# mLSTM scan of a hybrid decoder layer: the state unpadded, the query product per head in alternating halves of TensorE's array, key sums for two heads and score row sums for a row tile in one matmul each

## The chip, the cores and the metric

One core of a Trainium2 chip runs one launch of one layer of a hybrid decoder: TensorE for the matmuls, VectorE, ScalarE and GpSimd beside it, DMA queues for the weights. The metric is the device time of a launch in microseconds (us), the median of some runs; lower is better.

## The reference, cut to what matters

The sequence is 256 tokens, the model width 2048. Behind an RMSNorm and one wide projection stand three token mixers (forgetting attention, gated DeltaNet, mLSTM), whose outputs are gated, summed and projected; a gated MLP with a short convolution and a final RMSNorm follow. The change is in the mLSTM, a scan over 4 chunks of 64 tokens, for 8 heads with keys and queries of 64 and values of 128 numbers. In shortened form:

```
def step(carry, xs):                 # per chunk of L = 64 tokens
    C, n, m = carry                  # C (h, 64, 128), n (h, 64)
    ...
    Sm = Wd * qk_i                   # masked, weighted scores, 64 x 64 per head
    num = w_inter[..., None] * einsum('bhld,bhde->bhle', q_i, C) + einsum('bhls,bhse->bhle', Sm, v_i)
    den = w_inter * einsum('bhld,bhd->bhl', q_i, n) + sum(Sm, axis=-1)
    h = num / maximum(abs(den), exp(-m_r))[..., None]
    C = w_inter[..., -1, None, None] * C + einsum('bhl,bhld,bhle->bhde', wL, k_i, v_i)
    n = w_inter[..., -1, None] * n + einsum('bhl,bhld->bhd', wL, k_i)
```

## The kernel before

The weights stream through a ring of four slots in chunks of 128 x 1024 numbers. ScalarE rounds each to a high part `w_hi`, VectorE or GpSimd takes the low part `w_lo`, and TensorE multiplies both with the activations `xnT`, in groups of 128 x 512 outputs. These are the groups `ps<-w_hi,xnT` and `ps<-w_lo,xnT` in the rows. They make up most of the program.

The token mixers are cut into small *items*, which `plan_items()` places behind numbered weight chunks, so that TensorE does a projection, then an item, then a projection. The order of all items is fixed when the program is built. Items take turns in two pairs of PSUM banks, banks 4 and 5 and banks 6 and 7; `item_done` and `item_free` hand them over between TensorE and the engine that reads the result. `item(k)` is a function of each engine's program and issues what that engine does for item k.

Items of the mLSTM scan, per chunk c (rows `r` = partitions 0 to 63 for an even chunk and 64 to 127 for an odd one; `tt` = c // 2 is the row tile of 128 tokens):

- `qc` (from chunk 1 on): query times state. The queries `mq` hold a pair of heads on the partitions (even head on 0 to 63, odd head on 64 to 127). The state `c_st` is padded: for each pair of heads a block of 2 x 128 columns, in which the columns of the even head are zero on the odd head's partitions and the other way round. So one matmul with 128 rows and 256 columns gives both heads of a pair, 4 of them per chunk.
- `dc`: what the chunk adds to the state and to the norm. First, from chunk 1 on, 4 matmuls of queries with the key-sum state `n_st` (2 columns). Then for each of the 8 heads: the row sums of the scores `smt` (a matmul with a column of ones, 1 column), the sum of the weighted keys `mkt` (1 column), and keys times values `mkt`, `mv` (128 columns). All three have 64 rows and 64 output partitions: `smt` writes the partitions `r`, the other two write those of the head's half. VectorE then forms `den`, scales the state by `w_last` into `c_n` (two operations, one per half of the partitions) and adds the new part into `c_st` (two more), and raises `mstate_ready`, for which the next `qc` waits.
- `sv` (after an odd chunk, two weight chunks later): scores times values for the whole row tile.

The next `qc` follows four weight chunks behind a `dc`. The names in a row such as `ps<-c_st,mq` are written tile <- moving operand, stationary operand. A shape as `128*64` is rows x columns of the array that a matmul takes up. Each fp32 matmul of the program stands as two records in the trace, each with a weight load of its own, so "x8" in a row is 4 matmuls of the code.

```
                elif name == "qc":
...
                    for j in range(H // 2):
                        last = mm(oh[r, 2 * j:2 * j + 2, :], mq[:, j, c * L:c * L + L], c_st[:, j, :, :])
```

Of the kernel before, what the change touches and what calls it, by code (L numbers as in the profile page):

```python
# [14 lines left out]
ALU = mybir.AluOpType  # L15
# [5 lines left out]
P = 128  # L21
# [3 lines left out]
NT = SEQ // P  # L25
# [143 lines left out]
def hybrid_layer_kernel(nc, x, norm_mix_g, w_in, fox_f_bias, gdn_conv_w, gdn_a_log, gdn_dt_bias, gdn_norm_g,  # L169
# [3 lines left out]
    with ctx:  # L173
        cursor = [nc.sbuf_base + (-nc.sbuf_base) % 2048]

        def small(name, shape, dt=F32):
            n = 4
            for s in shape[1:]:
                n *= s
            at = cursor[0]  # L180
            cursor[0] += n + (-n) % 64
            return nc.alloc_sbuf_tensor_at(name, shape, dt, offset=at)
# [48 lines left out]
        c_kw = small("c_kw", [P, NT, H])  # L231
        w_last = small("w_last", [P, NT, 2, H])
        n_st = small("n_st", [P, H // 2, 2])
# [65 lines left out]

        c_st = part("c_st", 0, [P, H // 2, 2, HD])  # L300
        c_n = part("c_n", 2, [P, H // 2, HD])
        mt1 = part("mt1", 1, [P, H, HD])
# [135 lines left out]

        BLOCKS = (slice(0, L), slice(L, P))

        def within(ap, b):
# [134 lines left out]
        def _(pe):  # L576
# [86 lines left out]
            def item(k):  # L663
# [152 lines left out]
                elif name == "qc":  # L816
                    c, = args
                    r, tt = chunk_rows(c)
                    pe.wait_ge(S["mstate_ready"], c)
                    for j in range(H // 2):  # L820
                        last = mm(oh[r, 2 * j:2 * j + 2, :], mq[:, j, c * L:c * L + L], c_st[:, j, :, :])
                elif name == "dc":
# [6 lines left out]
                    if c:  # L829
                        for j in range(H // 2):  # L830
                            mm(o[r, 1, 2 * j:2 * j + 2], mq[:, j, c * L:c * L + L], n_st[:, j, :])
                    for h in range(H):
                        g = slice(L * (h % 2), L * (h % 2) + L)
                        j = h // 2
                        mm(o[r, 1, 8 + h:9 + h], smt[r, tt, h, r], ones[r, 0:1])
                        mm(o[g, 1, 16 + j:17 + j], mkt[r, tt, h, :], ones[r, 0:1])
                        last = mm(o[g, 0, j * P:j * P + P], mkt[r, tt, h, :], mv[r, tt, h, :])
                elif name == "sv":
# [454 lines left out]
        def _(dve):  # L1293
# [50 lines left out]
            def item(k):  # L1344
# [137 lines left out]
                elif name == "mtail":  # L1482
                    item_written(dve, k)
                    dve.tensor_copy(w_last[:, :, :, :].rearrange("p t b h -> p b t h"),
                                    o[:, 0, 16:48].rearrange("p (b t h) -> p b t h", b=2, t=2))
                    tt_(c_kw[:, :, :], vs[:, :, :], o[:, 0, 0:16].rearrange("p (t h) -> p t h", t=2),
# [21 lines left out]
                elif name == "qc":  # L1508
# [3 lines left out]
                    if c == 2:  # L1512
                        item_read(dve, "sv", 0)
                    tt_(mt1[r, :, :], oh[r], over_free(w_int8[r, tt, :], HD), ALU.mult).then_inc(free, 1)
                elif name == "dc":
# [4 lines left out]
                    if c == 0:  # L1520
                        chain(dve.tensor_copy(den[r, tt, :], o[r, 1, 8:16]))
                        dve.wait_ge(S["ml_zero"], 3)
                        for b in range(2):
                            g = slice(L * b, L * b + L)
                            dve.tensor_copy(n_st[g, :, b], o[g, 1, 16:20])
                            ins = dve.tensor_copy(c_st[g, :, b, :], dcs[g])
                        chain(ins)
                    else:
                        item_read(dve, "qc", c)
                        chain(tt_(den[r, tt, :], o[r, 1, 0:8], w_int8[r, tt, :], ALU.mult))  # L1530
                        chain(tt_(den[r, tt, :], den[r, tt, :], o[r, 1, 8:16], ALU.add))
                        for b in range(2):
                            g = slice(L * b, L * b + L)
                            wl = w_last[g, tt, c % 2, :].rearrange("p (j b) -> p j b", b=2)[:, :, b]
                            tt_(c_n[g, :, :], c_st[g, :, b, :], over_free(wl, HD), ALU.mult)
                            chain(tt_(n_st[g, :, b], n_st[g, :, b], wl, ALU.mult))
                        for b in range(2):
                            g = slice(L * b, L * b + L)
                            tt_(n_st[g, :, b], n_st[g, :, b], o[g, 1, 16:20], ALU.add)
                            ins = tt_(c_st[g, :, b, :], c_n[g, :, :], dcs[g], ALU.add)  # L1540
                        chain(ins)
                    dve.sem_inc(S["mstate_ready"], 1)
# [334 lines left out]
        def _(pool):  # L1877
# [54 lines left out]
            def item(k):  # L1932
# [31 lines left out]
                elif name == "vbc":  # L1964
                    tt, = args
                    if tt == 0:
                        item_written(pool, k)
                        for t in (n_st[:, :, :], c_st[:, :, :, :], mt1[:, :, :]):
                            pool.memset(t, 0.0).then_inc(S["ml_zero"], 1)
# [78 lines left out]
```

## Time and profile before

| What | us |
|---|---|
| Median of 3 runs | 1839.68 |
| Lowest and highest of them | 1837.96, 1841.13 |
| Span of the profiled execution (first to last instruction) | 1838.6 |
| TensorE busy in it, matmuls | 1817.3 (99%) |
| TensorE weight loads, beside the matmuls | 1567.1 (85%) |
| VectorE, ScalarE, GpSimd busy | 1065.3, 826.7, 434.0 |

The profile is of one execution; its page gives a span and no separate time, and the span lies 1.1 us under the median of the runs. A timeline row gives the start from the beginning of the span, the length of the group, the engine, the line, the operation with its tiles, the array shape, the shape of the output and the number of records.

### The profile page before, as it was taken

To read this page: it belongs to the slowest core of one execution; us is meant where nothing else is said; L and a number is where in the kernel's file an instruction comes from. 1 tells how busy PE (TensorE), PEld (TensorE's weight loads), DVE (VectorE), ACT (ScalarE), POOL (GpSimd) and SP (SyncE) were. 2 spreads that over 40 slices of the span, in tenths; PEclk is the share of its full clock that TensorE was granted. 3 is DMA by queue.
4 is the path that set the end of the run, shared out by engine and by line. 5 is a ranking of instruction groups with operands and counts; after the bars stand their busy time and mean duration, and the time that the engine had idled before them with its cause. 6 is when DMAs were issued, how large, how long until landed. Compare 5 with 4: busy or idle time off the path is not lost.

```text
span 1838.6 us, 28288 instructions
## 1 busy us (share of the span) xinstructions
PE 1817.3 (99%) x10949; PEld 1567.1 (85%) x10949; DVE 1065.3 (58%) x1279; ACT 826.7 (45%) x910; POOL 434.0 (24%) x242
## 2 busy tenths in 40 slices
PE   8999999999999999999999999999999999999997
PEld 6888898888888888888888878888888888888886
DVE  5678736366555755555556366666666666633334
ACT  5555333436433544444444354444444444444444
POOL 5222431121221222222222232222222222222223
PEclk9999999999999999999999999999999999999999
DMA  6666544444554566666667646666666666665663
GB/s 199 178 180 180 148 116 135 130 138 139 165 154 121 155 207 182 197 192 184 188 188 244 202 148 185 183 190 190 189 184 190 188 191 184 213 195 186 196 194 134
DMA packets 263436, 324.58 MB, mean 177 GB/s; under 512 B 16779, under 2 KB 230213, under 8 KB 262725
## 3 DMA queue, kind: packets, MB, share of 16 engines
q1 hardware_dynamic: 263366, 323.58, 58.2%
q8 instruction: 51, 0.84, 0.2%
q14 instruction: 19, 0.16, 0.0%
HBM read 321.45 MB, written 2.10 MB: 176 GB/s over the span
## 4 chain that ended last, share of the span: by engine, by line
PE 97%; DVE 1%; ACT 1%; DMA 0%; issue 0%; DVEq 0%; SPq 0%; ACTq 0%
PE ps L578 96%; PE ps L659 0%; DVE xs L1808 0%; DMA x_in<-in_x_dram 0%; PE ps L690 0%; PE ps L872 0%; PE ps L849 0%; ACT w_hi L376 0%; ACT p L994 0%; DVE x L1791 0%; ACT junk L994 0%; ACT x_sq L994 0%; PE ps L955 0%; DVE fmax L1448 0%; DVE p L1443 0%
## 5 line engine op out<-in xcount | busy, mean ns | idle before, releaser
L376 ACT ACTIVATE w_hi<-raw 128x1024 fp32r<-128x1024 f32 x601 | 635.1, 1059 | 877.5 <-PE ps L578 866.4
L381 DVE TENSOR_TENSOR w_lo<-raw,w_hi 128x1024 fp32r<-128x1024 f32 x450 | 561.5, 1254 | 490.7 <-ACT w_hi L376 489.8
L578 PE MATMUL ps<-xnT,w_hi 128*128 128x512 f32 (+1 forms) x2960 | 748.7, 394 | 0.7 <-issue 0.7
L381 POOL TENSOR_TENSOR w_lo<-raw,w_hi 128x1024 fp32r<-128x1024 f32 x151 | 366.7, 2428 | 1305.6 <-ACT w_hi L376 1305.6
L578 PEld LDWEIGHTS ps<-xnT,w_hi 128*128 128x128 f32 (+1 forms) x2960 | 532.4, 189 | 99.4 <-issue 1.5
L578 PEld LDWEIGHTS ps<-xnT,w_lo 128*128 128x128 f32 (+1 forms) x2960 | 403.9, 190 | 29.0
L578 PE MATMUL ps<-xnT,w_lo 128*128 128x256 f32 (+1 forms) x2960 | 415.2, 282 | 0.0
L578 PE MATMUL ps<-w_hi,xnT 128*128 128x512 f32 x1408 | 356.4, 392 | 0.0
L578 PEld LDWEIGHTS ps<-w_hi,xnT 128*128 128x128 f32 x1408 | 261.8, 188 | 54.7 <-issue 0.7
L578 PE MATMUL ps<-w_lo,xnT 128*128 128x512 f32 x704 | 192.2, 389 | 0.0
L578 PEld LDWEIGHTS ps<-w_lo,xnT 128*128 128x128 f32 x704 | 132.1, 188 | 27.8 <-DVE w_lo L381 0.2
L1342 DVE TENSOR_REDUCE upre<-ps 128x512 f32<-128x1024 f32 x44 | 53.9, 1224 | 136.9 <-PE ps L578 136.9
L1848 DVE SCALAR_TENSOR_TENSOR uacc<-upre,fconv_c,uacc 128x256 f32<-128x256 f32 x176 | 77.5, 481 | 11.8 <-DVE uacc L1846 0.2
L1342 DVE TENSOR_REDUCE g_sum<-ps 128x512 f32<-128x1024 f32 x24 | 29.3, 1221 | 28.9 <-PE ps L578 28.9
L1342 DVE TENSOR_REDUCE g_pr<-ps 128x512 f32<-128x1024 f32 x24 | 29.3, 1221 | 28.2 <-PE ps L578 28.2
L994 ACT ACT_TABLE_LOAD x30 | 38.5, 1283 | 1.3 <-PEq L2036 0.8
L994 ACT ACTIVATE g_sig<-g_sum,cols 128x256 f32<-128x256 f32 x48 | 21.9, 503 | 26.9 <-DVEq L1624 21.8
L1606 DVE SCALAR_TENSOR_TENSOR acc<-pre,conv_c,acc 128x256 f32<-128x256 f32 x72 | 32.5, 492 | 1.3
L578 PE MATMUL ps<-y_gdn,w_hi 128*128 128x512 f32 x128 | 32.1, 392 | 0.0
L578 PE MATMUL ps<-y_ml,w_hi 128*128 128x512 f32 x128 | 32.1, 392 | 0.0
L578 PE MATMUL ps<-y_fox,w_hi 128*128 128x512 f32 x128 | 32.0, 392 | 0.0
L1929 POOL TENSOR_TENSOR nlv<-nt,level 128x512 f32<-128x512 f32 x12 | 18.9, 1586 | 39.7 <-PE ps L578 33.5
(325 smaller groups left out, 1031.0 us busy)
## 6 DMA issues: line engine op xcount, KB each, us to landing
raw<-in_w_in_dram SPq DMA_DIRECT2D x256, 512.0 KB, 3.8
raw<-in_w_up_dram SPq DMA_DIRECT2D x176, 512.0 KB, 3.9
raw<-in_w_down_dram SPq DMA_DIRECT2D x88, 512.0 KB, 4.4
raw<-in_w_out_dram SPq DMA_DIRECT2D x32, 512.0 KB, 4.5
raw<-in_w_fox_proj_dram SPq DMA_DIRECT2D x16, 512.0 KB, 4.2
raw<-in_w_gdn_proj_dram SPq DMA_DIRECT2D x16, 512.0 KB, 4.3
raw<-in_w_ml_proj_dram SPq DMA_DIRECT2D x16, 512.0 KB, 4.0
x_in<-in_x_dram SPq DMA_DIRECT2D x4, 512.0 KB, 6.0
```

The costliest lines, as they stand in the source:

```text
L376: act.activation(w_hi[:, s, 0:n], raw[:, s, 0:n], ACT.Copy).then_inc(hi_ready[s], 1)
L381: eng.tensor_tensor(w_lo[:, s, 0:n], raw[:, s, 0:n], w_hi[:, s, 0:n], ALU.subtract).then_inc(lo_ready[s], 1)
L578: return pe.matmul(o, l, r, start=start, stop=stop)
L994: return act.activation(o, i, fn, **kw)
L1342: return dve.tensor_reduce(dst, ps[:, b0:b0 + 2, :].rearrange("p b (s t) -> p b t s", s=2), AX.X, ALU.add)
L1606: ins = dve.scalar_tensor_tensor(acc[:, b, :], pre[:, b, j:j + SEQ], conv_c[:, j, n:n + 1], acc[:, b, :], ALU.mult, ALU.add)
L1848: ins = dve.scalar_tensor_tensor(uacc[:, w, b, :], src, cw, uacc[:, w, b, :], ALU.mult, ALU.add)
L1929: pool.tensor_tensor(nlv[:, tt, :, :], nt_[:, tt, :, :], over_heads(level[:, lv, 0:L], H), ALU.mult).then_inc(S["level_ready"], 1)
```

## The change

Five things, all in the mLSTM scan:

1. `c_st` loses its padding (128 x 4 x 128 in place of 128 x 4 x 2 x 128), and `c_n` goes. GpSimd no longer clears `c_st`.
2. `qc` is 8 matmuls, one per head, of 64 rows, 64 output partitions and 128 columns, with even heads on array rows 0 to 63 and odd heads on 64 to 127 in turn. Even heads write one PSUM bank and odd heads the other (`by_half`).
3. The score row sums are taken once for a row tile, in its even chunk, with 128 rows and 128 output partitions: 8 matmuls in chunks 0 and 2, none in 1 and 3.
4. The key sums are taken for a pair of heads at a time: 4 matmuls per chunk with 64 rows and 128 output partitions, in place of 8 with 64.
5. VectorE scales and adds the state over all 128 partitions at once and in place: 2 operations of 128 x 512 in place of 4 of 64 x 512. `w_last` holds only the heads of a partition's half.

The numbers of keys-times-values matmuls and of queries-times-`n_st` matmuls stay as they were, and so does the order of items and weight chunks.

```diff
-        c_st = part("c_st", 0, [P, H // 2, 2, HD])
-        c_n = part("c_n", 2, [P, H // 2, HD])
+        c_st = part("c_st", 0, [P, H // 2, HD])
...
+        def by_half(oh):
+
+            return oh.rearrange("p (b j) d -> p j b d", b=2)
...
                     pe.wait_ge(S["mstate_ready"], c)
-                    for j in range(H // 2):
-                        last = mm(oh[r, 2 * j:2 * j + 2, :], mq[:, j, c * L:c * L + L], c_st[:, j, :, :])
+                    for h in range(H):
+                        g = BLOCKS[h % 2]
+                        last = mm(by_half(oh)[r, h // 2, h % 2, :], mq[g, h // 2, c * L:c * L + L], c_st[g, h // 2, :])
...
                     if c:
                         for j in range(H // 2):
                             mm(o[r, 1, 2 * j:2 * j + 2], mq[:, j, c * L:c * L + L], n_st[:, j, :])
+                    if c % 2 == 0:
+                        for h in range(H):
+                            mm(o[:, 1, 8 + h:9 + h], smt[:, tt, h, :], ones[:, 0:1])
+                    for j in range(H // 2):
+                        mm(o[:, 1, 16 + j:17 + j], mkt[r, tt, 2 * j:2 * j + 2, :].rearrange("p b l -> p (b l)"), ones[r, 0:1])
                     for h in range(H):
-                        g = slice(L * (h % 2), L * (h % 2) + L)
                         j = h // 2
-                        mm(o[r, 1, 8 + h:9 + h], smt[r, tt, h, r], ones[r, 0:1])
-                        mm(o[g, 1, 16 + j:17 + j], mkt[r, tt, h, :], ones[r, 0:1])
-                        last = mm(o[g, 0, j * P:j * P + P], mkt[r, tt, h, :], mv[r, tt, h, :])
+                        last = mm(o[BLOCKS[h % 2], 0, j * P:j * P + P], mkt[r, tt, h, :], mv[r, tt, h, :])
...
                         item_read(dve, "qc", c)
-                        chain(tt_(den[r, tt, :], o[r, 1, 0:8], w_int8[r, tt, :], ALU.mult))
-                        chain(tt_(den[r, tt, :], den[r, tt, :], o[r, 1, 8:16], ALU.add))
-                        for b in range(2):
-                            g = slice(L * b, L * b + L)
-                            wl = w_last[g, tt, c % 2, :].rearrange("p (j b) -> p j b", b=2)[:, :, b]
-                            tt_(c_n[g, :, :], c_st[g, :, b, :], over_free(wl, HD), ALU.mult)
...
+                        dve.tensor_tensor(den2[r, tt, :], o[r, 1, 0:8], w_int8[r, tt, :], ALU.mult)
+                        if c % 2 == 0:
+                            dve.tensor_copy(den[:, tt, :], o[:, 1, 8:16])
+                        wl = w_last[:, tt, c % 2, :]
+                        tt_(c_st[:, :, :], c_st[:, :, :], over_free(wl, HD), ALU.mult)
...
+                        chain(tt_(c_st[:, :, :], c_st[:, :, :], dcs, ALU.add))
                     dve.sem_inc(S["mstate_ready"], 1)
```

On TensorE, the items `qc` and `dc` of chunk 1 stood as follows before, counted in matmuls of the code, between two projections (the numbers behind the names are the program's buffer numbers):

```order
L578 MATMUL ps<-w_lo_51,xnT_52 128x512 x4
L578 MATMUL ps<-c_st_147,mq_141 64x256 x4
L578 MATMUL ps<-n_st_94,mq_141 64x2 x4
L578 MATMUL ps<-ones_54,smt_146 64x1
L578 MATMUL ps<-ones_54,mkt_143 64x1
L578 MATMUL ps<-mv_144,mkt_143 64x128
```

The last three rows repeat for each of the 8 heads, and a projection follows. In the changed kernel the same place reads:

```order
L581 MATMUL ps<-w_lo_51,xnT_52 128x512 x4
L581 MATMUL ps<-c_st_147,mq_141 64x128 x8
L581 MATMUL ps<-n_st_94,mq_141 64x2 x4
L581 MATMUL ps<-ones_54,mkt_143 128x1 x4
L581 MATMUL ps<-mv_144,mkt_143 64x128 x8
L581 MATMUL ps<-w_hi_50,xnT_52 128x512 x8
```

The interleaved one-column matmuls have become runs of one kind, and the score sums have left this odd chunk. Chunk 2, an even one, holds them for its row tile, on TensorE of the changed kernel:

```order
L581 MATMUL ps<-c_st_147,mq_141 64x128 x8
L581 MATMUL ps<-n_st_94,mq_141 64x2 x4
L581 MATMUL ps<-ones_54,smt_146 128x1 x8
L581 MATMUL ps<-ones_54,mkt_143 128x1 x4
L581 MATMUL ps<-mv_144,mkt_143 64x128 x8
```

Before, chunk 2 was the same as chunk 1. Now it has 8 score sums with 128 output partitions between the `n_st` matmuls and the key sums.

## Rows read from the trace of the kernel before

**Rows 1.** the page: span, busy time of each engine, chain by engine
```profile
span 1838.6 us, 28288 instructions
...
PE 1817.3 (99%) x10949; PEld 1567.1 (85%) x10949; DVE 1065.3 (58%) x1279; ACT 826.7 (45%) x910; POOL 434.0 (24%) x242
...
PE 97%; DVE 1%; ACT 1%; DMA 0%; issue 0%; DVEq 0%; SPq 0%; ACTq 0%
...
```

**Rows 2.** windows: length; busy (x) PE, PEld, DVE, ACT, POOL; granted clock; DMA share; GB/s
```profile
...
1087.40:1090.80 3.40, 1.09 (x8) 0.86 (x8) 3.27 (x3) 2.20 (x5) 3.40 (x3) 1.00 0.21 56
1090.80:1097.70 6.90, 5.36 (x19) 4.00 (x20) 6.90 (x8) 5.01 (x8) 3.05 (x3) 0.51 0.15 51
...
545.00:595.00 50.00, 50.00 (x365) 41.27 (x364) 28.25 (x54) 15.93 (x15) 7.17 (x3) 1.00 0.45 129
...
```

**Rows 3.** timeline of TensorE, chunk 0: start, length, group xrecords
```profile
...
533.81 1.07 PE L578 MATMUL ps<-w_lo,xnT 128*128 128x512 f32 x4
534.81 0.27 PE L578 MATMUL ps<-ones,smt 64*64 64x1 f32 x2
...
537.25 2.14 PE L578 MATMUL ps<-w_hi,xnT 128*128 128x512 f32 x8
...
```

**Rows 4.** timeline of TensorE, chunk 1
```profile
...
548.40 1.94 PE L578 MATMUL ps<-c_st,mq 128*64 128x256 f32 x8
550.18 0.58 PE L578 MATMUL ps<-n_st,mq 128*64 128x2 f32 x8
550.68 0.21 PE L578 MATMUL ps<-ones,smt 64*64 64x1 f32 x1
550.69 0.21 PE L578 MATMUL ps<-ones,mkt 64*64 64x1 f32 x1
...
553.10 2.11 PE L578 MATMUL ps<-w_hi,xnT 128*128 128x512 f32 x8
...
```

**Rows 5.** timeline of TensorE, chunk 2
```profile
...
566.00 1.94 PE L578 MATMUL ps<-c_st,mq 128*64 128x256 f32 x8
...
570.72 2.11 PE L578 MATMUL ps<-w_hi,xnT 128*128 128x512 f32 x8
...
```

**Rows 6.** timeline of TensorE, chunk 3
```profile
...
581.83 1.94 PE L578 MATMUL ps<-c_st,mq 128*64 128x256 f32 x8
...
586.52 2.11 PE L578 MATMUL ps<-w_hi,xnT 128*128 128x512 f32 x8
...
```

**Rows 7.** timeline of TensorE, short matmuls on the whole array
```profile
...
493.41 1.07 PE L578 MATMUL ps<-w_lo,xnT 128*128 128x512 f32 x4
494.32 0.28 PE L578 MATMUL ps<-m_t,sel 128*128 128x8 f32 x2
494.45 2.08 PE L578 MATMUL ps<-w_hi,xnT 128*128 128x512 f32 x8
...
507.19 0.60 PE L578 MATMUL ps<-w_int,sel 128*128 128x16 f32 x4
507.63 1.07 PE L849 MATMUL ps<-ident,gvt 128*128 128x128 f32 x8
...
```

**Rows 8.** timeline of TensorE, item u (64x64 tiles) and item wt
```profile
...
324.32 2.00 PE L578 MATMUL ps<-xmt,kbg 64*128 64x64 f32 x32
326.25 2.11 PE L578 MATMUL ps<-w_hi,xnT 128*128 128x512 f32 x8
...
334.08 1.96 PE L578 MATMUL ps<-gvt,xmt 64*64 64x128 f32 x32
335.97 2.14 PE L578 MATMUL ps<-w_hi,xnT 128*128 128x512 f32 x8
...
```

**Rows 9.** timeline of TensorE, item mqk (row halves)
```profile
...
517.74 1.16 PE L578 MATMUL ps<-mq,mk 64*128 64x128 f32 x16
518.83 1.09 PE L659 MATMUL ps<-ident,bm 128*128 128x128 f32 x8
...
```

**Rows 10.** timeline of VectorE, end of chunk 1's state update
```profile
...
557.27 0.20 DVE L1546 RECIPROCAL rd<-den 64x8 f32<-64x8 f32 x1
...
```

More of the change, by code:

```diff
@@ L231, in hybrid_layer_kernel @@
         c_kw = small("c_kw", [P, NT, H])
-        w_last = small("w_last", [P, NT, 2, H])
+        w_last = small("w_last", [P, NT, 2, H // 2])
         n_st = small("n_st", [P, H // 2, 2])
@@ L1483, in item @@
                     item_written(dve, k)
-                    dve.tensor_copy(w_last[:, :, :, :].rearrange("p t b h -> p b t h"),
-                                    o[:, 0, 16:48].rearrange("p (b t h) -> p b t h", b=2, t=2))
+                    for b, g in enumerate(BLOCKS):
+                        dve.tensor_copy(w_last[g, :, :, :].rearrange("p t c j -> p c t j"),
+                                        o[g, 0, 16:48].rearrange("p (c t j b) -> p c t j b", c=2, t=2, b=2)[:, :, :, :, b])
                     tt_(c_kw[:, :, :], vs[:, :, :], o[:, 0, 0:16].rearrange("p (t h) -> p t h", t=2),
@@ L1513, in item @@
                         item_read(dve, "sv", 0)
-                    tt_(mt1[r, :, :], oh[r], over_free(w_int8[r, tt, :], HD), ALU.mult).then_inc(free, 1)
+                    w8 = w_int8[r, tt, :].rearrange("p (j b) -> p j b", b=2)
+                    tt_(mt1[r, :, :].rearrange("p (j b) d -> p j b d", b=2), by_half(oh)[r],
+                        w8.unsqueeze(3).to_broadcast([L, H // 2, 2, HD]), ALU.mult).then_inc(free, 1)
                 elif name == "dc":
@@ L1520, in item @@
                     if c == 0:
-                        chain(dve.tensor_copy(den[r, tt, :], o[r, 1, 8:16]))
-                        dve.wait_ge(S["ml_zero"], 3)
-                        for b in range(2):
-                            g = slice(L * b, L * b + L)
+                        dve.tensor_copy(den[:, tt, :], o[:, 1, 8:16])
+                        dve.wait_ge(S["ml_zero"], 2)
+                        for b, g in enumerate(BLOCKS):
                             dve.tensor_copy(n_st[g, :, b], o[g, 1, 16:20])
-                            ins = dve.tensor_copy(c_st[g, :, b, :], dcs[g])
@@ L1527, in item @@
-                        chain(ins)
+                        chain(dve.tensor_copy(c_st[:, :, :], dcs))
                     else:
                         item_read(dve, "qc", c)
-                        chain(tt_(den[r, tt, :], o[r, 1, 0:8], w_int8[r, tt, :], ALU.mult))
-                        chain(tt_(den[r, tt, :], den[r, tt, :], o[r, 1, 8:16], ALU.add))
-                        for b in range(2):
-                            g = slice(L * b, L * b + L)
-                            wl = w_last[g, tt, c % 2, :].rearrange("p (j b) -> p j b", b=2)[:, :, b]
-                            tt_(c_n[g, :, :], c_st[g, :, b, :], over_free(wl, HD), ALU.mult)
-                            chain(tt_(n_st[g, :, b], n_st[g, :, b], wl, ALU.mult))
@@ L1537, in item @@
-                        for b in range(2):
-                            g = slice(L * b, L * b + L)
+                        dve.tensor_tensor(den2[r, tt, :], o[r, 1, 0:8], w_int8[r, tt, :], ALU.mult)
+                        if c % 2 == 0:
+                            dve.tensor_copy(den[:, tt, :], o[:, 1, 8:16])
+                        wl = w_last[:, tt, c % 2, :]
+                        tt_(c_st[:, :, :], c_st[:, :, :], over_free(wl, HD), ALU.mult)
+                        for b, g in enumerate(BLOCKS):
+                            ins = tt_(n_st[g, :, b], n_st[g, :, b], wl[g], ALU.mult)
@@ L1539, in item @@
+                        chain(ins)
+                        tt_(den[r, tt, :], den[r, tt, :], den2[r, tt, :], ALU.add)
+                        for b, g in enumerate(BLOCKS):
                             tt_(n_st[g, :, b], n_st[g, :, b], o[g, 1, 16:20], ALU.add)
-                            ins = tt_(c_st[g, :, b, :], c_n[g, :, :], dcs[g], ALU.add)
-                        chain(ins)
+                        chain(tt_(c_st[:, :, :], c_st[:, :, :], dcs, ALU.add))
                     dve.sem_inc(S["mstate_ready"], 1)
@@ L1967, in item @@
                         item_written(pool, k)
-                        for t in (n_st[:, :, :], c_st[:, :, :, :], mt1[:, :, :]):
+                        for t in (n_st[:, :, :], mt1[:, :, :]):
                             pool.memset(t, 0.0).then_inc(S["ml_zero"], 1)
```

## The prediction

> **What bounds the kernel now.** I read the page first: TensorE is busy for 1817.3 of 1838.6 us and makes up 97% of the chain that ended last [rows 1]. Then the windows: from 545 to 595 us, where the scan lies, TensorE is busy for all 50.00 us, VectorE for 28.25, at full granted clock [rows 2]. So within the scan nothing but TensorE's own time counts: a microsecond less in an item starts the next projection a microsecond sooner, and what VectorE saves counts for nothing. Last I read TensorE's timeline chunk by chunk, from the item's first record to the first record of the next projection: chunk 0 takes 537.25 - 534.81 = 2.44 us [rows 3], chunk 1 553.10 - 548.40 = 4.70 [rows 4], chunk 2 570.72 - 566.00 = 4.72 [rows 5], chunk 3 586.52 - 581.83 = 4.69 [rows 6]. Together 16.55 us, 0.9% of the span: the change can touch no more than that. Within chunk 1, `qc` takes 550.18 - 548.40 = 1.78 us for 8 records, the `n_st` products 0.50 for 8, and the rest 553.10 - 550.68 = 2.42 us for 48 records (16 each of score sums, key sums and keys times values) [rows 4].
>
> **Prices from the rows.** Durations in the rows overlap, so a price is the distance between starts.
> (a) A record of few columns on 64 array columns: 0.50 / 8 = 0.06 us [rows 4].
> (b) A record of few columns on 128 array columns: the four `w_int` records go from 507.19 to 507.63, 0.11 us each, at 16 columns [rows 7]. That the columns of the weights set it and not the rows is seen in item wt: 32 records of 64 rows on 128 array columns, in alternating row halves, take 326.25 - 324.32 = 1.93 us, 0.12 per pair, though they stream 64 columns only [rows 8].
> (c) Pairs of 64x64 tiles side by side at 128 columns: item u has 32 records in 335.97 - 334.08 = 1.89 us [rows 8]. Half is 0.95; the ends don't halve, so I take 1.0 for 16 records. Item mqk says the same for row halves that write the same PSUM partitions in two banks, as the new `qc` does, but on 128 array columns: 16 records in 518.83 - 517.74 = 1.09 us [rows 9].
> (d) Changing the array's shape: four `w_lo` records are followed after 534.81 - 533.81 = 1.00 us by a 64x64 record [rows 3] and after 494.32 - 493.41 = 0.91 by one on the whole array [rows 7]. So 0.09 us per change of shape.
>
> **The Trainium skill on this.** The rows (b) and (a) stand at 0.11 and 0.06 us for a record of few columns, so a merged sum on 128 array columns costs what two on 64 cost [rows 4, 7]. The Trainium skill ("TensorE: Matmul & The Clock Gate", section "LDWEIGHTS (loading the stationary operand)") states that a weight load lasts as long as its columns at 1.2 GHz, whatever the rows: 107 ns for 128. The trace agrees, with 112 ns; it speaks against merging sums. By its figure the 64 new sum records would be 64 x 0.005 = 0.3 us cheaper than by the rows, an estimate of -0.9 us in all in place of the -0.6 below.
>
> **The change, part by part.**
> *`qc`* (chunks 1 to 3): 8 records of 256 columns become 16 of 128 columns in two row halves. By (c) 1.0 us in place of 1.78, so -0.78 a chunk. The next group, the `n_st` products, now follows a change of shape at its head, which I put at 0.05 more in it: 0.55. This is the estimate nearest to (d); the end of `qc` is in the 1.0. Bounds: 8 steps of 0.11 us are the least that 2 x 128 columns allow by u and mqk (0.9), and without any overlap 16 records at half of 0.22 (1.78 / 8) give 1.78, no gain.
> *Score sums*: 16 records per chunk on 64x64 in four chunks go, 16 records on the whole array in chunks 0 and 2 come. By (b) 16 x 0.11 = 1.76 us, in each of the two. In chunk 0 they follow the projection without a change of shape (-0.09), and the first two start within 0.13 together (494.45 - 494.32 [rows 7]), so 1.7 there; in chunk 2 a change of shape is added (1.76 + 0.09 = 1.85).
> *Key sums*: 8 records per chunk, 64 rows on 128 array columns, all on the same rows, so one after the other: 8 x 0.11 = 0.88, and a change of shape 0.07 to 0.09: 0.95.
> *Keys times values*: the same 16 records, now without one-column records between. They alternate in columns only. By (c) 1.0 us if column halves run side by side as row halves do. They do in the trace: a `smt` record starts at 550.68 and an `mkt` record on the same rows and the other columns at 550.69 [rows 4]. The length of the old chunk says so too: 32 short records at 0.06 and 16 at 0.11 in a line would be 3.7 us, and it takes 2.42.
> *VectorE*: two operations fewer per chunk. The chain of chunk 1 ends at 557.27 + 0.20 us [rows 10], and the next `qc` starts at 566.00 [rows 5], so there are 8.5 us of room, and neither the shorter chain nor a `mt1` operation that reads its banks in another order is seen. GpSimd's clearing of `c_st` goes, worth nothing for the same reason: TensorE waits for neither. Were the cover gone, the whole chain of 557.47 - 553.10 = 4.4 us would stand on the path, three times.
>
> **The sum.**
> Chunk 0: -0.09 + 1.7 + 0.95 + 1.0 = 3.56, before 2.44: +1.12.
> Chunk 1: 1.0 + 0.55 + 0.95 + 1.0 = 3.50, before 4.70: -1.20.
> Chunk 2: 3.50 + 1.85 = 5.35, before 4.72: +0.63.
> Chunk 3: 3.50, before 4.69: -1.19.
> Total -0.64 us: what `qc` gains (3 x 0.73 = 2.2) is given back by the sums on 128 array columns, which no longer hide beside other tiles. The profiled span would be 1838.6 - 0.6 = 1838.0, and the median, 1.1 us above the span as before, 1839.68 - 0.6 = 1839.1. A measurement tells about 0.2%, or 3.7 us, from no change, so this is "the same".
>
> **Rivals.**
> *Short records on 128 array columns are cheap.* The 64 new sum records (16 in each of chunks 0 and 2, 8 in each of four chunks) would start 0.06 us apart as on 64 columns: 64 x 0.05 = 3.2 us less, -3.8 in all, 1835.9. If every one followed as closely as the second `m_t` record follows the first (two in 0.13 us, of which 0.11 is the last one's, leave 0.02 [rows 7]), it would be 64 x 0.09 = 5.8 less, 1833.3. The Trainium skill ("TensorEngine Tiling (Array Packing)", section "Instruction Overhead") has such a rule: a matmul of one column lasts as long as one of 60, about 60 cycles, or 25 ns at 2.4 GHz. Against it: the four `w_int` records at 0.11 [rows 7] and item wt [rows 8]. Chance 0.07; this is the faster side.
> *Column halves don't run side by side at 128 columns.* Keys times values would be 16 x 0.11 = 1.8 us in place of 1.0, +0.8 in four chunks, +3.2: total +2.6, 1842.3. For it: no row shows that kind of pair alone. The Trainium skill ("TensorE: Matmul & The Clock Gate", section "The mechanism") says that a weight load overlaps a running matmul only on other row groups. Against it: the two records 0.01 us apart and the length of the old chunk [rows 4]. Chance 0.08. If `qc` did not overlap either, +0.78 x 3 = 2.3 more and 1844.6, slower: chance 0.02.
> *The clock falls.* The new chunks 0 and 2 have 24 records of one column in a row, some 2.7 us in which little streams through the array. Where the clock did fall in this trace, TensorE had been busy for 1.09 of 3.40 us, and the stretch that followed had a mean of 0.51 for 6.9 us, the lower of the two levels, 1.2 GHz [rows 2]. That costs 3.4 us of work. Once, it gives +2.8 and 1842.5; in both chunks +6.2 and 1845.9, which decides for slower. Against it: before the fall TensorE stood idle, and here it does not; the `n_st` products and the interleaved sums of before left the clock at 1.00 [rows 2]. Chance 0.03, the slower half of it 0.02.
> *The gain comes from VectorE's shorter chain.* It would need a wait of TensorE on it, and the windows show none [rows 2]: chance 0.02, time then unknown but below the forecast.
>
> **How the numbers follow.** Forecast 0.78, with a range of its own from -2.5 us (the key sums and half of the score sums cheap) to +1.5 (the ends dearer in the 8 more changes of shape: 19 in place of 11): 1837 to 1841. The runs of before spread by 3.2 us, so a median moves by 1 to 2 by itself. The 80% range takes in the near end of the first rival and the second: 1835.5 to 1842.5. Faster by over 0.2%: the first rival 0.05 (most of its 0.07) plus 0.02 for what I don't see; slower by over 0.2%: 0.02 + 0.02 + 0.01; the same: 0.88.
>
> **What would show it.** In the timeline of the changed kernel: `c_st,mq` on 64*64 with 16 records and about 1.0 us to the first `n_st` record; `ones,smt` on 128*128 with 16 records and 1.7 to 1.85 us; `ones,mkt` on 64*128 with 8 records and 0.95; `mv,mkt` with 16 records and 1.0; chunks of 3.6, 3.5, 5.35 and 3.5 us with the granted clock at 1.00 throughout. The prediction is wrong if the sums on 128 array columns stand much under 0.11 us each, if keys times values take 1.8, or if a stretch at half clock appears.

## The result and the profile after

| | Median (lowest to highest), us | Runs |
|---|---|---|
| Before | 1840.0 (1837.96 to 1842.43) | 11 |
| Changed | 1844.13 (1842.5 to 1847.93) | 11 |

The changed kernel is slower: ratio 1.0028, 95% interval 1.002 to 1.0036, or about 4.1 us more. The forecast was 1839.1 with a range up to 1842.5, so it was wrong in the sign and in the range.

The page of the changed kernel, as [rows 1] of before:

```profile
span 1841.7 us, 28201 instructions
...
PE 1820.0 (99%) x10909; PEld 1570.6 (85%) x10909; DVE 1061.3 (58%) x1274; ACT 827.0 (45%) x910; POOL 432.1 (23%) x241
...
PE 97%; DVE 1%; ACT 1%; DMA 0%; issue 0%; DVEq 0%; SPq 0%; ACTq 0%
...
```

Nothing here names a cause. TensorE is as busy as before and has 40 records fewer, but 2.7 us more busy time. The timeline of TensorE names it, here chunk 0 (as [rows 3]):

```profile
...
532.50 1.84 PE L581 MATMUL ps<-ones,smt 128*128 128x1 f32 x16
534.27 1.05 PE L581 MATMUL ps<-ones,mkt 64*128 64x1 f32 x8
535.25 1.86 PE L581 MATMUL ps<-mv,mkt 64*64 64x128 f32 x16
537.04 3.78 PE L581 MATMUL ps<-w_hi,xnT 128*128 128x512 f32 x8
...
542.29 1.99 PE L581 MATMUL ps<-w_hi,xnT 128*128 128x512 f32 x8
```

The score sums take 534.27 - 532.50 = 1.77 us, the key sums 0.98, both as forecast. Then keys times values take 1.79 us, and the 8 records of the projection behind them 3.78 us, where the same group took 2.14 before [rows 3]. Chunk 1 (as [rows 4]) has none of this:

```profile
...
550.56 1.09 PE L581 MATMUL ps<-c_st,mq 64*64 64x128 f32 x16
551.58 0.63 PE L581 MATMUL ps<-n_st,mq 128*64 128x2 f32 x8
552.14 1.05 PE L581 MATMUL ps<-ones,mkt 64*128 64x1 f32 x8
553.12 1.09 PE L581 MATMUL ps<-mv,mkt 64*64 64x128 f32 x16
554.14 2.11 PE L581 MATMUL ps<-w_hi,xnT 128*128 128x512 f32 x8
```

It takes 554.14 - 550.56 = 3.58 us (forecast 3.50, before 4.70): query product 1.02, `n_st` 0.56, key sums 0.98, keys times values 1.02. Chunk 2 (as [rows 5]):

```profile
...
567.04 1.09 PE L581 MATMUL ps<-c_st,mq 64*64 64x128 f32 x16
568.06 0.63 PE L581 MATMUL ps<-n_st,mq 128*64 128x2 f32 x8
568.62 1.95 PE L581 MATMUL ps<-ones,smt 128*128 128x1 f32 x16
570.50 1.05 PE L581 MATMUL ps<-ones,mkt 64*128 64x1 f32 x8
571.48 1.09 PE L581 MATMUL ps<-mv,mkt 64*64 64x128 f32 x16
572.50 3.41 PE L581 MATMUL ps<-w_hi,xnT 128*128 128x512 f32 x8
...
```

5.46 us to the projection (forecast 5.35, before 4.72), and again a projection of 3.41 us behind it. The windows of the changed kernel over these places, with TensorE's busy time first and its granted clock after the five engines (as [rows 2]):

```profile
...
532.50:535.25 2.75, 2.75 (x26) 2.72 (x24) 1.23 (x1) 1.06 (x1) 0.00 (x0) 1.00 0.82 257
535.40:542.23 6.83, 6.83 (x28) 5.44 (x27) 1.59 (x7) 0.00 (x0) 0.00 (x0) 0.50 0.30 86
545.00:567.00 22.00, 22.00 (x137) 18.24 (x135) 11.27 (x18) 8.66 (x8) 3.47 (x2) 1.00 0.49 144
572.95:576.36 3.41, 3.41 (x10) 2.63 (x9) 2.32 (x10) 0.00 (x0) 0.00 (x0) 0.50 0.00 0
530.00:600.00 70.00, 70.00 (x433) 58.98 (x432) 30.36 (x58) 21.00 (x20) 9.57 (x4) 0.93 0.45 133
...
```

From 535.40 to 542.23 and from 572.95 to 576.36 us the granted clock is 0.50: 1.2 GHz, the lower of its two levels. TensorE is busy in all of both stretches and in all of the 2.75 us ahead of the first. What it did in these 2.75 us was 24 records of one column, back to back. The second stretch begins 0.45 us into the projection behind chunk 2, whose item has the same 24 records in it. In the 22 us between, with chunk 1 inside, the clock is 1.00. The two stretches are 10.24 us at half clock, so 5.1 us of work is lost. This one view names the place; that the columns of those records are the cause is what the experiments below have to show.

Counted from the first sum record of chunk 0 to the first projection behind the last `sv` (534.81 to 593.80 before, 532.50 to 596.04 after), the scan is 58.99 us long before and 63.54 after: +4.55. Without the 5.1 us, it would be 58.42: -0.57. The profiled spans differ by less than the scans, by 3.2 us, mostly because the scan of the changed kernel starts 2.31 us sooner (532.50 against 534.81). That differs from execution to execution: e2 and e6 below are the same up to the scan, and theirs start at 532.73 and 534.68. So from here on scans are compared, and not whole profiles.

### The profile page after: what moved, and what is told of

Read it like the earlier page. It is cut to its first block, busy times and chain, and to the rows that moved or that the text cites. A ratio compares the mean times of both kernels' runs of the same rounds, so it can differ in the third digit from the quotient of the medians.

```text
span 1841.7 us, 28201 instructions
## 1 busy us (share of the span) xinstructions
PE 1820.0 (99%) x10909; PEld 1570.6 (85%) x10909; DVE 1061.3 (58%) x1274; ACT 827.0 (45%) x910; POOL 432.1 (23%) x241
## 4 chain that ended last, share of the span: by engine, by line
PE 97%; DVE 1%; ACT 1%; DMA 0%; issue 0%; DVEq 0%; SPq 0%; ACTq 0%
PE ps L581 96%; PE ps L662 0%; DVE xs L1815 0%; DMA x_in<-in_x_dram 0%; PE ps L693 0%; PE ps L878 0%; PE ps L855 0%; ACT w_hi L375 0%; ACT p L1000 0%; DVE x L1798 0%; ACT junk L1000 0%; ACT x_sq L1000 0%; PE ps L961 0%; DVE fmax L1454 0%; DVE p L1449 0%
```

## The experiments

All of these are timed beside the kernel before on the same chip. For the scan of each profile, "scan" is the length as counted above, "low" the time in it at half clock, and "net" is scan less half of low. "Lower in" is the number of runs whose mean clock over the whole program was 0.995 or less. The kernel before has that in 12 of its 91 runs beside e1 to e12, 5 of them at 0.994. The median of before was 1840.35 us beside e1 to e4, 1841.13 beside e5 to e8, 1840.54 beside e9 to e12 and 1840.56 beside e13 and e14; the ratios are to these.

"Lower in" is a rough sign and no count of falls in the scan. Each profile here, that of before too, is at half clock over its last 4 to 7 us and in a stretch that begins between 1087 and 1101 us, where TensorE has idle time ahead of it [rows 2]. This stretch lasted 6.83 us before and in the changed kernel, 3.41 in e1, e10 and e12, and 10.24 in e2, e3, e4, e7 and e14. A run's mean clock counts all of this with the scan: the profiled run of e11 has a fall in the scan and still a mean of 0.996. The three lengths near 1090 us differ by up to 3.4 us of work, whatever the scan does, which blurs a gain of 2 us in the medians.

| Kernel | Median, us | Ratio to before (95%) | Scan | Low | Net | Lower in |
|---|---|---|---|---|---|---|
| before | 1840.0 | 1 | 58.99 | 0 | 58.99 | |
| changed | 1844.13 | 1.0028 (1.002 to 1.0036) | 63.54 | 10.24 | 58.42 | 11 of 11 |
| e1 query part alone | 1838.81 | 0.9996 (0.9987 to 1.0005) | 56.88 | 0 | 56.88 | 5 of 11 |
| e2 key sums merged, score sums old | 1845.95 | 1.0025 (1.0016 to 1.0034) | 66.82 | 17.07 | 58.29 | 11 of 11 |
| e3 score sums merged, key sums old | 1840.98 | 1.0004 (0.9995 to 1.0013) | 60.15 | 6.83 | 56.74 | 8 of 11 |
| e4 changed, both sums 96 columns | 1840.03 | 0.9998 (0.9989 to 1.0007) | 59.24 | 0 | 59.24 | 0 of 11 |
| e5 diagonal score sums, 48 columns | 1837.19 | 0.9983 (0.9974 to 0.9992) | 55.74 | 0 | 55.74 | 0 of 11 |
| e6 as e2, key sums 96 columns | 1844.13 | 1.0017 (1.0008 to 1.0026) | 65.40 | 13.65 | 58.58 | 9 of 10 |
| e7 as e1, heads grouped | 1843.33 (one run) | | 59.97 | 3.41 | 58.26 | 1 of 1 |
| e8 changed, score sums 96 columns | 1839.7 | 0.9995 (0.9985 to 1.0004) | 58.95 | 0 | 58.95 | 0 of 10 |
| e9 as e1, both sums 48 columns | 1838.71 | 0.9991 (0.9982 to 1.0) | 56.88 | 0 | 56.88 | 0 of 12 |
| e10 as e2, score sums 48 columns | 1844.14 | 1.0022 (1.0013 to 1.0031) | 63.57 | 10.24 | 58.45 | 10 of 10 |
| e11 as e5, one column | 1837.84 | 0.9988 (0.998 to 0.9997) | 57.24 | 3.41 | 55.53 | 2 of 12 |
| e12 changed, key sums last | 1846.99 | 1.0036 (1.0021 to 1.005) | 63.56 | 10.24 | 58.44 | 6 of 6 |
| e13 merged sums alone | 1847.46 | 1.0031 (1.002 to 1.0043) | 68.91 | 17.07 | 60.37 | 7 of 7 |
| e14 as e2, both sums wider | 1839.89 | 1.0001 (0.9992 to 1.001) | 60.75 | 3.41 | 59.04 | 3 of 10 |

**e1: the query part alone.** Score sums and key sums are put back as before, the rest of the change stays.

```diff
-                    if c % 2 == 0:
-                        for h in range(H):
-                            mm(o[:, 1, 8 + h:9 + h], smt[:, tt, h, :], ones[:, 0:1])
-                    for j in range(H // 2):
-                        mm(o[:, 1, 16 + j:17 + j], mkt[r, tt, 2 * j:2 * j + 2, :].rearrange("p b l -> p (b l)"), ones[r, 0:1])
                     for h in range(H):
                         j = h // 2
+                        mm(o[r, 1, 8 + h:9 + h], smt[r, tt, h, r], ones[r, 0:1])
+                        mm(o[BLOCKS[h % 2], 1, 16 + j:17 + j], mkt[r, tt, h, :], ones[r, 0:1])
                         last = mm(o[BLOCKS[h % 2], 0, j * P:j * P + P], mkt[r, tt, h, :], mv[r, tt, h, :])
...
```

(VectorE reads the score sums per chunk again.) The causes that the expectations set against each other are: theory A, too few columns stream through the array; rival B, the changes of array shape; rival C, the per-head query product or the vector part; and, from e4 on, rival D, the weight loads themselves.

> The changed kernel with the score row sums and the key sums put back as before, per head and on 64x64 tiles between keys times values; the unpadded state, the per-head query product and VectorE's wider operations stay. Theory A (the two runs of one-column records on 128 array columns in chunks 0 and 2 let TensorE's clock fall): no stretch at half clock in the scan; chunk 0 stays at 2.44 us, chunks 1 to 3 take 1.02 + 0.56 + 2.42 = 4.0 in place of 4.7, so 2.1 us less than the kernel before: 1837.9 where that has 1840.0. Rival B (the changes of array shape lower the clock): this kernel has 14 against 11 before and 19 in the changed one, so no or one fall; 1837.9 to 1840. Rival C (the per-head query product or the vector part lowers it): the two falls stay, 1842.6.

Chunk 1 in its timeline of TensorE, and the window over its scan (busy times, then the granted clock):

```profile
...
548.68 1.09 PE L581 MATMUL ps<-c_st,mq 64*64 64x128 f32 x16
549.70 0.63 PE L581 MATMUL ps<-n_st,mq 128*64 128x2 f32 x8
...
552.67 0.50 PE L581 MATMUL ps<-w_hi,xnT 128*128 128x512 f32 x1
...
530.00:600.00 70.00, 70.00 (x532) 59.21 (x531) 34.32 (x64) 24.08 (x23) 10.79 (x5) 1.00 0.51 148
...
```

552.67 - 548.68 = 3.99 us, as expected, and the scan is 2.11 us shorter with no stretch at half clock in it. The median, though, is only 1.5 us under that of before (1838.81 to 1840.35), which can't be told from no change, and 5 of 11 runs have a mean clock of 0.994. The price of the query part is settled here, its worth in time is not.

**e2 and e3: one of the merged sums at a time.** e2 puts back the score sums, e3 the key sums, each with its line of e1's diff.

> The changed kernel with the score row sums put back per head on 64x64 tiles; key sums stay merged on 128 array columns. The longest run of short records is then that of chunk 1 of the changed kernel (8 query-times-key-sum and 8 key sum records, 1.5 us), in which its clock held. Theory A: no fall; key sums 0.98, score sums and keys times values together 1.8 us, so chunk 0 takes 2.8 (+0.35), the others 4.4 (-0.34 each): 0.7 less than before, 1839.3. Rival B (changes of shape, here 17): one or two falls, 1841 to 1844. Rival C: two falls, 1844.

> The changed kernel with the key sums put back per head on 64x64 tiles; score row sums stay merged in chunks 0 and 2. Short runs are 1.8 us in chunk 0 and 2.4 us in chunk 2, between the 1.5 us that kept the clock and the 2.7 and 3.4 us behind which it fell. By the prices of the changed kernel, key sums and keys times values take 1.3 us together, chunks 3.0, 2.9, 4.8, 2.9: 2.9 less than before, 1837.1 if the clock holds. Theory A says no more than that the fall gets rarer or shorter than in the changed kernel: 1837 to 1841. Rival B (13 changes of shape): no fall, 1837.1. Rival C: two falls, 1842.

e2 refutes theory A as first put. It has no merged score sums and falls in all four chunks. Its windows, the granted clock after the five engines:

```profile
...
536.61:540.02 3.41, 3.41 (x9) 2.64 (x8) 0.74 (x4) 0.00 (x0) 0.00 (x0) 0.50 0.42 141
553.68:557.09 3.41, 3.41 (x10) 2.67 (x9) 2.16 (x10) 0.00 (x0) 0.00 (x0) 0.50 0.12 46
570.75:577.57 6.82, 6.82 (x33) 5.83 (x30) 2.92 (x13) 0.00 (x0) 0.00 (x0) 0.50 0.28 79
591.22:594.64 3.42, 3.42 (x10) 2.64 (x9) 2.41 (x10) 0.00 (x0) 0.00 (x0) 0.50 0.07 23
...
```

17.07 us at half clock lose 8.5 us, and the rest of its scan is 0.7 us shorter than before, just as expected. e3 falls in chunks 0 and 2, for 3.41 us each. Its net scan is 2.25 us shorter than before, where 2.9 was expected: key sums with keys times values were put at 1.3 us, and in e5, which has them the same way, they take 537.67 - 536.14 = 1.53. Against e1 the net scans also say what each merge costs: merged key sums 1.41 us (e2), merged score sums nothing (e3, 0.14 less).

Rival B is not settled by these two, and the counts in the expectations are off: by the order of shapes e2 has 18 changes, e3 15 and e12 19, not 17, 13 and 18. What settles it is e4, with the changes of the changed kernel.

**e4 and e8: the same records, more columns.** In the changed kernel the moving operand of the sums gets 96 equal columns for one (e4 for both sums, e8 for the score sums alone). The surplus sums land in columns that the next matmul overwrites or that nobody reads.

```diff
-                            mm(o[:, 1, 8 + h:9 + h], smt[:, tt, h, :], ones[:, 0:1])
+                            mm(o[:, 1, 8 + h:104 + h], smt[:, tt, h, :], ones[:, 0:96])
...
-                        mm(o[:, 1, 16 + j:17 + j], mkt[r, tt, 2 * j:2 * j + 2, :].rearrange("p b l -> p (b l)"), ones[r, 0:1])
+                        mm(o[:, 1, 16 + j:112 + j], mkt[r, tt, 2 * j:2 * j + 2, :].rearrange("p b l -> p (b l)"), ones[r, 0:96])
```

> The changed kernel in which every score sum and key sum streams 96 equal columns in place of 1 (the surplus sums land in columns of the bank that nobody reads or that the next matmul overwrites; the outputs are the same). Same number and size of weight loads, same changes of shape, same order; by the weight loads' 0.112 us per record the runs last as long. Theory A (too little streams): the two stretches at half clock go, chunks 3.7, 3.6, 5.5, 3.6 us, time within 0.5 of the kernel before: 1839.7. Rival B (changes of shape) and rival D (the weight loads themselves): the falls stay, 1844.

> The changed kernel with 96 columns streamed in the score sums alone; the key sums stay at one column. Theory A: chunks 0 and 2 then have a one-column run no longer than that of chunk 1 in the changed kernel, where the clock held, so no fall: 1840.0, as with both widened. If the key sums' run is enough, as e2 suggests, falls stay in some chunks: 1842 to 1844.

Chunk 0 of e4 in the timeline of TensorE, to be read against chunk 0 of the changed kernel above:

```profile
...
532.60 1.92 PE L581 MATMUL ps<-ones,smt 128*128 128x96 f32 x16
534.45 1.13 PE L581 MATMUL ps<-ones,mkt 64*128 64x96 f32 x8
535.51 1.09 PE L581 MATMUL ps<-mv,mkt 64*64 64x128 f32 x16
536.53 0.73 PE L581 MATMUL ps<-w_hi,xnT 128*128 128x512 f32 x2
```

The score sums last 1.85 us (1.77 with one column) and the key sums 1.06 (0.98), though they stream 96 times as much. Keys times values are back at 1.02 us. The window over the whole scan of e4 has the clock at 1.00, where the changed kernel had 0.93:

```profile
...
530.00:600.00 70.00, 70.00 (x459) 59.23 (x458) 32.75 (x61) 22.28 (x21) 9.57 (x4) 1.00 0.49 141
...
```

None of 21 runs of e4 and e8 has a mean clock under 0.996, where the changed kernel had 0.991 to 0.995 in all 11, and their medians are within noise of the kernel before. Number and size of weight loads, changes of shape and order are the same as in the changed kernel, so rivals B and D fall. Columns streamed and columns written to PSUM grow together in this edit; no run tells them apart. For the changed kernel, the columns of the score sums alone are enough to keep the clock.

**e6, e10 and e14: widening in e2.** e6 widens the key sums of e2 (96 columns), e10 its score sums (48), e14 both, with the same kind of edit; where score sums are widened behind the key sums, the latter get columns of their own.

> The kernel of e2 (score row sums per head on 64x64 tiles, key sums merged on 128 array columns), the key sums streaming 96 equal columns in place of 1. Same records, same loads. If the key sums' run together with what stands beside it starves the array, as theory A has it, the four falls of e2 go and 1839.6 is left (0.7 under the kernel before). If the loop of score sums and keys times values behind it is what lowers the clock, the falls stay: 1843 to 1846.

> The kernel of e2 with the score row sums in its loop streaming 48 equal columns, the key sums left at one: the counterpart of e6, which widened the key sums alone and kept three falls. Theory A': the loop of 16 score sum and 16 keys-times-values records, most of them on one quarter of the array, is what streams least in e2; widened, the falls get rarer, 1839.5 to 1841.5. If the merged key sums' run is what counts, they stay: 1844 to 1846.

> The kernel of e2 with both kinds of sums streaming more equal columns (score sums 48, key sums 96), where e6 and e10 widened one kind each and kept three falls. If what streams in the item as a whole decides (A'), the falls go: 1839.8. If something else in this order of records lowers the clock (the score sums and half of the keys-times-values products on one quarter of the array), they stay: 1842 to 1846.

With one kind widened, three chunks fall in either profile and the medians stay 3.0 and 3.6 us above that of before. With both, the median is 1839.89 (0.7 under before), as expected, but one fall remains in the profile and 3 of 10 runs have a lower clock. So most of e2's falls come from both kinds of narrow records together, as far as one profile of each kernel tells; what is behind the one that remains, in chunk 3, is open.

**e9: e1 with wider sums.** The sums of e1 stream 48 columns.

> The kernel of e1 (query product per head in alternating halves, both sums per head on 64x64 tiles) with the sums streaming 48 equal columns in place of 1. The records stay 0.058 us apart by their weight loads, so the items should last as long: chunks 2.4, 4.0, 4.0, 4.0. Theory A': what decides is how much streams in an item as a whole, and the shorter query product left e1 short of it, which shows in the lower clock of 5 of its 11 runs. Then no run here has a fall and the median is 2.1 us under the kernel before: 1838.4. If the falls of e1 have another cause (rival C, the per-head query product itself), the spread stays as in e1 and the median near 1.5 under.

The scan is 56.88 us, as in e1 to the hundredth. No run of 12 has a mean clock of 0.995 or less, and their spread falls to 1837.02 to 1839.57 (e1: 1835.86 to 1843.13). The median is not better than e1's, though: 1838.71, 1.8 under before. The interval, 0.9982 to 1.0, just reaches no change. That e1's lower clocks come from its narrow sums is likely by these counts (5 of 11 against 0 of 12), but no profile shows where in the program they lie; that they cost its median anything is not shown.

**e7: does the alternation matter?** The loop of e1's query product runs over the heads 0, 2, 4, 6, 1, 3, 5, 7.

```diff
-                    for h in range(H):
+                    for h in (0, 2, 4, 6, 1, 3, 5, 7):
                         g = BLOCKS[h % 2]
```

> The kernel of e1 with the heads of the query product in the order 0, 2, 4, 6, 1, 3, 5, 7, so that consecutive matmuls lie on the same half of the array. If the alternation is what makes it cheap (two row halves side by side), the query product takes 16 records at 0.107 = 1.7 to 1.8 us again in place of 1.02, 0.7 more in each of chunks 1 to 3. If the unpadded state alone were enough, it stays at 1.02.

Chunk 1 in its timeline of TensorE:

```profile
...
549.08 1.58 PE L581 MATMUL ps<-c_st,mq 64*64 64x128 f32 x16
550.58 0.63 PE L581 MATMUL ps<-n_st,mq 128*64 128x2 f32 x8
...
```

1.50 us, between the two values expected. The alternation is worth 0.48 us a chunk. It is still cheaper than 1.7: in the middle of the group, from 549.56 to 549.95, the trace has 8 records that start 0.05 us apart on average, and 0.11 or more apart at both ends, so two tiles run side by side there. Its one run, 1843.33, says nothing of the time.

**e12: cut the run.** In the changed kernel the key sums move behind keys times values.

```diff
-                    for j in range(H // 2):
-                        mm(o[:, 1, 16 + j:17 + j], mkt[r, tt, 2 * j:2 * j + 2, :].rearrange("p b l -> p (b l)"), ones[r, 0:1])
                     for h in range(H):
                         j = h // 2
-                        last = mm(o[BLOCKS[h % 2], 0, j * P:j * P + P], mkt[r, tt, h, :], mv[r, tt, h, :])
+                        mm(o[BLOCKS[h % 2], 0, j * P:j * P + P], mkt[r, tt, h, :], mv[r, tt, h, :])
+                    for j in range(H // 2):
+                        last = mm(o[:, 1, 16 + j:17 + j], mkt[r, tt, 2 * j:2 * j + 2, :].rearrange("p b l -> p (b l)"), ones[r, 0:1])
```

> The changed kernel with the order score sums, keys times values, key sums in the item: the same records, 18 changes of shape for 19, but the run of 24 one-column records is cut into 16 and 8 with 1.0 us of keys times values between. If the unbroken run is what lowers the clock (theory A as first put), the falls go or get rare: 1840 to 1841.5. If it is the amount streamed around the item as a whole (A'), they stay: 1843.5 to 1845.

Same falls, same 10.24 us, and a median of 1846.99 in six runs. An unbroken run of 24 is not what it takes. Theory A in its later form (A': what streams in the item as a whole decides) fits; how much an item must stream is not measured.

**e5 and e11: a version that gains.** Key sums as before; score sums once per row tile, but as pairs of 64x64 tiles on the diagonal. A semaphore orders them ahead of the rest of the item; no run leaves it out. e5 streams 48 columns, e11 one.

```diff
...
                     if c % 2 == 0:
                         for h in range(H):
-                            mm(o[:, 1, 8 + h:9 + h], smt[:, tt, h, :], ones[:, 0:1])
-                    for j in range(H // 2):
-                        mm(o[:, 1, 16 + j:17 + j], mkt[r, tt, 2 * j:2 * j + 2, :].rearrange("p b l -> p (b l)"), ones[r, 0:1])
+                            for b in BLOCKS:
+                                last = mm(o[b, 1, 8 + h:56 + h], smt[b, tt, h, b], ones[b, 0:48])
+                        last.then_inc(S["sums_done"], 1)
+                        pe.wait_ge(S["sums_done"], tt + 1)
                     for h in range(H):
                         j = h // 2
+                        mm(o[BLOCKS[h % 2], 1, 16 + j:17 + j], mkt[r, tt, h, :], ones[r, 0:1])
                         last = mm(o[BLOCKS[h % 2], 0, j * P:j * P + P], mkt[r, tt, h, :], mv[r, tt, h, :])
```

> Key sums as before, per head on 64x64 tiles between keys times values; score row sums once per row tile, in chunks 0 and 2, but as 64x64 tiles on the diagonal of the array (rows 0-63 to partitions 0-63 beside rows 64-127 to partitions 64-127), streaming 48 equal columns, and closed with a semaphore ahead of the rest of the item. 16 pairs of records at 0.058 us and a drain of some 0.2 make 1.1 us in chunks 0 and 2; odd chunks take 3.11 us as with merged score sums and old key sums. Chunks 2.6, 3.1, 4.2, 3.1: 3.5 us less than before. If the clock holds, as more streams per microsecond than in the changed kernel: 1836.8. If a short run of records is by itself enough for a fall (rivals B and D): one or two falls, 1838.5 to 1840.5.

> The kernel of e5 with one column per score sum in place of 48. Same records and waits, so 1837.2 if the clock holds. Theory A': it streams less in chunks 0 and 2 than any kernel here that held its clock in every run, so falls appear: median 1838 to 1841. If short records on 64x64 tiles don't count (only those on 128 array columns do), no falls and 1837.2.

Chunk 0 of e5 in the timeline of TensorE:

```profile
...
534.93 1.14 PE L581 MATMUL ps<-ones,smt 64*64 64x48 f32 x32
536.14 0.28 PE L581 MATMUL ps<-ones,mkt 64*64 64x1 f32 x4
...
537.67 1.21 PE L581 MATMUL ps<-w_hi,xnT 128*128 128x512 f32 x4
```

32 records take 1.21 us with the wait at their end, where 16 on the whole array took 1.77. The scan is 3.25 us shorter and at full clock in the profile, none of the 11 runs has a mean clock under 0.996, and the median is 1837.19 against 1841.13: ratio 0.9983, 0.9974 to 0.9992, a small gain but clear of noise. It is 3.9 us under the kernel before, and some 7 under the changed one, which was timed apart from it. With one column (e11) the profile shows one fall, in chunk 0, and 2 other runs of the 12 have a lower clock; the median of 1837.84 is under the range expected for falls. So narrow records on 64x64 tiles can be followed by a fall too, but falls are rarer or shorter there than I expected. The interval of e11 lies under 1 as well.

**e13: the merged sums alone.** The kernel before, with padded state and paired query product, and the sums of the changed kernel.

> The kernel before with the merged sums alone: padded state and paired query product stay, score row sums and key sums are as in the changed kernel. By the prices measured there, chunk 0 3.7 and the others 0.76 longer than in the changed kernel, 1.5 us more than before without a fall. If the merged sums lower the clock by themselves, falls in chunk 0 at least: 1843 to 1845. If it takes the shorter query product as well (its share of the cause), no fall: 1842.0.

It has the highest median, 1847.46, though not apart from e12's 1846.99 in so few runs. Its window over the scan, the clock 0.89:

```profile
...
530.00:610.00 80.00, 80.00 (x434) 65.94 (x433) 37.29 (x68) 23.09 (x22) 9.77 (x5) 0.89 0.42 124
...
```

It falls in all four chunks. So the merged sums lower the clock by themselves, and rival C falls: neither the shorter query product nor the new vector part is needed for it. Net of the clock the scan is 1.4 us longer than before (expected 1.5).

## Why the prediction was wrong

- **TensorE bounds the scan, VectorE's part is worth nothing**: right. TensorE is busy for 70.00 of 70.00 us in the scan of the changed kernel, and the chunks differ by TensorE's terms alone. The vector part was not timed by itself.
- **Query product** (-0.73 a chunk with the group behind it): right. 1.02 + 0.56 us where the sum had 1.0 + 0.55; alone it takes 2.11 us off the scan (e1), 0.70 a chunk, and the alternation makes 0.48 us of each chunk's (e7).
- **Score sums at 0.11 us a record, key sums 0.95**: right. 1.77 and 1.88 us (forecast 1.7 and 1.85), and 0.98. The first rival is gone: the records start 0.11 us apart at one column as they do at 96 (e4), and 0.06 apart on 64 array columns, so the columns of the weights set the price.
- **Keys times values in column halves side by side**: right, 1.02 us. The second rival is gone.
- **The sum**, -0.64 us: right net of the clock. The scan's net length is 0.57 shorter, 0.66 with the change of shape ahead of chunk 0 (0.09), which the count leaves out. As forecast, what the query product gains goes into the sums.
- **The step that failed** is in the rival on the clock, which got a chance of 0.03: "before the fall TensorE stood idle, and here it does not; the `n_st` products and the interleaved sums of before left the clock at 1.00". I took a stretch without idle time for a safe one, and so put a cost at next to nothing that came to 5.1 us of work. It isn't safe: TensorE was busy by its records in every microsecond ahead of both falls. With the same loads at the same pace the clock fell or held by the columns streamed: no run of e4 and e8 shows the changed kernel's low clock, four chunks fall in e2 and one in e14, and 5 of 11 runs of e1 have a lower clock against none of e9. The second half of the argument compared the wrong thing too. The old sums stood between products of 128 columns and beside a second tile; in the changed kernel they stand together, and nothing streams beside them. e13 shows that this exchange alone brings the falls. Which of its parts does is argued, not tested.
- **The price of that rival** was near. It had 3.4 us for each of two falls, 1845.9 in all. The profile has one stretch of 6.83 and one of 3.41 us, 5.1 us lost, and the median came to 1844.13. The runs vary with it: at a mean clock of 0.995 they take 1842.5 to 1844.7, at 0.991 1847.6 to 1847.9. The range should have reached this case.

The Trainium skill ("TensorE: Matmul & The Clock Gate", section "Loop structure matters more than you think") gives matmuls that stay back to back as the loop that stays warm. The trace does not agree: they were back to back, and the clock fell to 0.50. The measurement decides.

What stays open is why a kernel falls in one chunk and not in its twin (e6 and e10 in chunks 0, 1 and 3, not 2), and why some runs of before show a lower clock. For those at 0.995 a longer stretch near 1090 us would do: 10.24 us in place of 6.83 takes the mean from 0.9962 in the profile of before to 0.9953, an estimate from these lengths. Those at 0.994 need more. No run here tests either question.

## What to carry to other kernels

Merging small matmuls into one with more weight columns saved nothing here, where the weight load sets the pace, and it took away the wide work that hid them. When TensorE bounds a kernel, look at the granted clock behind every stretch of narrow matmuls, not only behind idle time: where records are paced by their weight loads, columns to spare in the moving operand cost almost nothing (0.08 us for 16 records) and kept the clock. Pairs of tiles on the diagonal of the array, as in e5, made the small sums cheaper than one matmul on all of it.

## What the runs showed of the hardware

- The granted clock of TensorE fell to half with TensorE busy without a gap: 10.24 us in the changed kernel's scan, 17.07 in e13's. More columns per record, at the same loads, kept it at 1.00 (e4, e8).
- Every stretch at half clock in the scans was 3.41 or 6.83 us long, and the one near 1090 us 3.41, 6.83 or 10.24; the 2.75 us of one-column records in chunk 0 of the changed kernel were followed by the longer one, which lost 3.4 us of work.
- A record on 128 array columns started 0.11 us after the last whether it streamed 1 or 96 columns (1.77 against 1.85 us for 16), and a short one on 64 array columns 0.06 us after.
- Tiles that share rows and differ in columns ran side by side at 128 columns: 16 records in 1.02 us, where the Trainium skill ("TensorE: Matmul & The Clock Gate", section "The mechanism") has weight loads overlap running matmuls only on other row groups.
